# Single-stream layer: the down product by seven half-size products, with the residual added by pairs of tiles

## The reference, cut to what matters

```python
def swiglu(h, w_gate, w_up, w_down):
    return (jax.nn.silu(h @ w_gate) * (h @ w_up)) @ w_down

x = x + token_mixing(x, ...)
h = rmsnorm(x, ffn_norm_g[l])
x = x + swiglu(h, ff_w_gate[0], ff_w_up[0], ff_w_down[0])   # l = 0
x = x + token_mixing(x, ...)                                 # l = 1, begins with rmsnorm(x)
```

## Time and profile before

| | |
|---|---|
| median of 3 runs | 3439.45 us (3438.46 to 3442.85) |
| the profiled execution | 3442.54 us |
| its span | 3440.5 us |
| TensorE busy | 3270.0 us, 95% |
| VectorE, ScalarE, POOL busy | 26%, 20%, 14% |
| mean granted TensorE clock | 0.963 of full |

### The profile page before, as it was taken

The page is one execution under the profiler, slowest core; times in us unless marked ns, Lnnn a source line. Parts: engine busy times, 40 slices in busy tenths (PEclk is TensorE's granted clock), DMA queues, the critical chain, the costliest instruction groups (busy, mean ns, idle before and its releaser), DMA issues.

```text
span 3440.5 us, 81881 instructions
## 1 busy us (share of the span) xinstructions
PE 3270.0 (95%) x35194; PEld 2864.3 (83%) x35195; DVE 897.4 (26%) x1990; ACT 691.1 (20%) x1505; POOL 495.7 (14%) x441
## 2 busy tenths in 40 slices
PE   7999789999899999999999999989999999999998
PEld 5886678888786788787799887778899999988888
DVE  2324745553313321214233123130000110011001
ACT  2324122221204321212211011201111211101011
POOL 1210125555121010100057010000000000000000
PEclk9999689999899999999999999989999999999999
DMA  6546012222233244343344442238999999944477
GB/s 274 198 165 233 3 49 83 88 85 88 72 104 123 88 157 137 125 141 110 110 160 156 150 147 98 97 124 338 381 380 396 388 394 378 402 151 149 143 271 290
DMA packets 94204, 638.90 MB, mean 186 GB/s; under 512 B 10720, under 2 KB 11760, under 8 KB 36480
## 3 DMA queue, kind: packets, MB, share of 16 engines
q1 hardware_dynamic: 91472, 628.62, 49.2%
q0 software_dynamic: 2608, 8.49, 0.8%
HBM read 636.02 MB, written 1.05 MB: 185 GB/s over the span
## 4 chain that ended last, share of the span: by engine, by line
PE 89%; DMA 4%; DVE 3%; ACT 2%; issue 2%; POOL 0%; SPq 0%; ACTq 0%; DVEq 0%
PE bank L1109 18%; PE bank L663 18%; PE bank L618 12%; PE bank L781 12%; PE bank L802 5%; PE bank L634 5%; PE bank L719 4%; PE bank L1069 2%; DMA ring<-in_moe_down 2%; PE bank L566 2%; PE bank L592 1%; PE bank L1124 1%; PE bank L838 1%; DMA ring<-in_moe_up 1%; PE bank L820 1%
## 5 line engine op out<-in xcount | busy, mean ns | idle before, releaser
L781 PE MATMUL bank<-PROJ,ring 128*64 128x80 f32 (+1 forms) x7424 | 485.0, 257 | 11.6 <-DMA ring<-in_moe_down 7.7
L1109 PE MATMUL bank<-MIX,ring 128*64 128x80 f32 x12544 | 473.7, 235 | 21.1 <-issue 10.9
L1109 PEld LDWEIGHTS bank<-MIX,ring 128*64 128x64 f32 x12544 | 448.6, 138 | 47.0 <-issue 39.7
L781 PEld LDWEIGHTS bank<-PROJ,ring 128*64 128x64 f32 (+1 forms) x7424 | 441.8, 145 | 53.5 <-DMA ring<-in_moe_down 12.5
L618 PE MATMUL bank<-H,ring 128*128 128x256 f32 x1856 | 407.5, 382 | 4.1 <-ACT H L1297 4.1
L618 PEld LDWEIGHTS bank<-H,ring 128*128 128x128 f32 x1856 | 354.4, 192 | 56.7 <-issue 4.7
L1109 PE MATMUL bank<-H,ring 128*128 128x256 f32 x896 | 193.7, 379 | 0.0
L663 PE MATMUL bank<-H,ring 128*64 128x128 f32 (+1 forms) x1296 | 185.2, 331 | 5.4 <-ACT H L1297 4.7
L1109 PEld LDWEIGHTS bank<-H,ring 128*128 128x128 f32 x896 | 170.2, 190 | 23.4 <-issue 0.3
L663 PE MATMUL bank<-MIX,ring 128*64 128x128 f32 (+1 forms) x1272 | 181.1, 321 | 0.8 <-DVE MIX L1884 0.8
L802 PE MATMUL bank<-H,ring 128*128 128x256 f32 x768 | 178.0, 390 | 3.9 <-ACT PROJ L1396 3.7
(11 more groups left out here) (383 smaller groups left out, 3717.4 us busy)
## 6 DMA issues: line engine op xcount, KB each, us to landing
ring<-in_moe_up SPq DMA_DIRECT2D x224, 1024.0 KB, 7.2
ring<-in_moe_down SPq DMA_DIRECT2D x128, 896.0 KB, 6.3
ring<-in_up SPq DMA_DIRECT2D x44, 1024.0 KB, 4.8
ring<-in_mod_b SPq DMA_DIRECT2D x40, 1024.0 KB, 6.5
ring<-in_tproj SPq DMA_DIRECT2D x32, 1024.0 KB, 4.8
ring<-in_proj SPq DMA_DIRECT2D x26, 1024.0 KB, 4.8
ring<-in_gates SPq DMA_DIRECT2D x24, 1024.0 KB, 4.8
ring<-in_swup SPq DMA_DIRECT2D x22, 1024.0 KB, 4.8
```

Source lines behind the costliest of these rows:

```text
L781: mm = pe.matmul(B[bank][lo:lo + m, 0:width], w[:, k, lo:lo + m], src(s * half + k), start=s == 0 and k == 0, stop=s == 1 and k == half - 1)
L1109: mm = pe.matmul(B[(t0 + 2 * j + t) % 4][lo:lo + m, 0:n], w[:, k, t * P + lo:t * P + lo + m], src[:, k, 0:n], start=k == 0, stop=k == KT - 1)
```

## The change

`swdown` joins the stages by seven: 12 units of 1024 KB instead of 16 of 704 KB. VectorE makes the token sums of chunks 0 and 1 before the last gating, chunk 2's after it. POOL makes the weight sums two units ahead. ScalarE copies out the four lone products, in one loop before the squares of norm 10. VectorE combines each pair of tiles and adds it to X in one operation of 512 columns, and the square sums stand at fixed places between. The squares of norm 10 move from H to SC, where they share four places (`square_home`), with a wait on the fourth and later squares (`square_free`).

```diff
-SEVEN = ('proj0', 'wout0', 'up0', 'down0', 'proj1', 'swup')
+SEVEN = ('proj0', 'wout0', 'up0', 'down0', 'proj1', 'swup', 'swdown')
...
-DOWNS = ('down0',)
+DOWNS = ('down0', 'swdown',)
...
                     seven("swup", "norm9_out")
-                    down("swdown", T, ("lin_free", tile_base["swup"] + 2 * FT + 4, 2))
+                    seven_down("swdown")
...
                     sqrt_table(eps)
+                    for j in range(4):
+                        seven_head("swdown", j)
                     squares(10, X, T, lin_free, tile_base["swdown"] + 5, 1)
...
                         c_sums(name, j, it)
+                        if j == FT - 1:
+                            down_sums("swdown", (0, 1))
...
-                    add_out(10, "swdown")
+                    down_sums("swdown", (2,))
+                    for j in range(4):
+                        c_sums("swdown", j)
+                        dve.wait_ge(S("sv_c"), result_at("swdown") + j + 1)
+                        x = X[:, 2 * j:2 * j + 2, 0:T]
+                        dve.tensor_tensor(x, x, flat(seven_parts("swdown", j)[0]).rearrange("p (k t) -> p k t", t=T), ALU.add)\
+                           .then_inc(lin_free, 2)
+                        for k in ((), (1,), (2, 3), (4, 5))[j]:
+                            sum_square(10, k, T)
+                    sum_square(10, 6, T)
...
                             sums_ahead("swup", j, it)
+                    for j in range(2):
+                        pool.wait_ge(unit_done, base["swup"] + FT - 1 + j)
+                        w_sums("swdown", j)
+                    for j in range(10):
+                        sums_ahead("swdown", j)
```

More of the change, by code:

```diff
@@ L28 @@
 MOD_A = 8
-SEVEN = ('proj0', 'wout0', 'up0', 'down0', 'proj1', 'swup')
-SEVEN_UNITS = {'proj0': 11, 'wout0': 4, 'up0': 22, 'down0': 12, 'proj1': 4, 'swup': 22}
-SEVEN_WIDTH = {'proj0': 512, 'wout0': 512, 'up0': 512, 'down0': 512, 'proj1': 512, 'swup': 256}
+SEVEN = ('proj0', 'wout0', 'up0', 'down0', 'proj1', 'swup', 'swdown')
+SEVEN_UNITS = {'proj0': 11, 'wout0': 4, 'up0': 22, 'down0': 12, 'proj1': 4, 'swup': 22, 'swdown': 12}
+SEVEN_WIDTH = {'proj0': 512, 'wout0': 512, 'up0': 512, 'down0': 512, 'proj1': 512, 'swup': 256, 'swdown': 256}
 CHUNKS = ((0, 4), (4, 4), (8, 3))
-DOWNS = ('down0',)
+DOWNS = ('down0', 'swdown',)
 MOD_P = 22
@@ L2080, in add_out @@
                         sum_square(n, k - 1, T)
[L2081 to L2086, removed]
+                    bank = B[(tile_base[name] + k) % 4]
+                    dve.wait_ge(*tile_in(name, k))
                     dve.tensor_tensor(X[:, k, 0:T], X[:, k, 0:T], bank[:, 0:T], ALU.add).then_inc(lin_free, 1)
@@ L2470, in layout @@
     out["swup"] = paired(f["ff_w_gate_2"][0], f["ff_w_up_2"][0])
-    out["swdown"] = down(f["ff_w_down_2"][0])
+    out["swdown"] = down_seven(f["ff_w_down_2"][0])
     out["moe_up"] = np.concatenate([paired(f["moe_w_gate_2"][0][e], f["moe_w_up_2"][0][e]) for e in range(N_EXPERTS)])
```

## The result

The changed kernel takes 3450.42 us (median of 6 runs, 3445.17 to 3452.65), the kernel before 3439.44 (median of 6, 3437.68 to 3448.09). The ratio is 1.0026, with a 95% interval of 1.0014 to 1.0038: slower, by 11 us between the medians (5 to 13 by the interval). Forecast was 3438.8 with a range up to 3445.0. The profiled execution took 3445.17 us, the shortest of the six, with a span of 3443.4.

What follows compares the result with a forecast made beforehand. TensorE was taken to bound the kernel, with 89% of the chain. Its work -8.9, the start +2.2 and the end +6.0 gave -0.7 us: 3438.8 us against the median of 3439.45, range 3432.5 to 3445.0.

Steps and rivals of the forecast that it cites:

- TensorE's work, -8.9 us: Single-stream down product: 1232 instructions at 54.6 ns, 67.2 us against 76.08, so 8.9 us less.
- Transfers: Down product's weights: 12 transfers of 1024 KB for 16 of 704 KB, each started early enough; no cost.
- POOL in steady state: Down product: POOL's weight sums keep up with at least 0.7 us to spare, so no wait.
- Rivals 3 and 4: Down product: POOL falls behind, 3444.9 us, chance 0.04; strips do not run side by side, 3505 us, chance 0.01.
- The start, +2.2: Down product's first units: VectorE's token sums take turns with POOL's weight sums and delay TensorE, 2.2 us more; bounds 0 and 4.
- The end, +6.0: Down product's end to small gates' end: late squares hold up VectorE's combinations, E + 18.0 against E + 11.95; bounds 3 and 7.
- rival 1, "ScalarE not late": Rival 1: stage's end or start is cheap, chance 0.24; its case of ScalarE not late at the end: 3435.8 us.
- The sum, -0.7: Whole kernel: work, start and end terms together make it 0.7 us faster, 3438.8 us against the median.
- Rival 2: New stage's straight code: instructions come too late, 9 issue waits add 19 us, 3458 us; chance 0.05.

Runs made afterwards that it cites:

- f3: Changed kernel, padding branched over and ScalarE's squares in turn, plus POOL's second-unit weight sums waiting for VectorE's chunk 0 sums: 3436.61 us, ratio 0.9988.
- e3: Changed kernel with ScalarE's lone copies and squares in turn, instead of all copies first: 3447.95 us, ratio 1.0021.
- e2: Kernel before the change, with 60 slots of redundant waits (120 waits) added on TensorE ahead of the router: 3457.85 us, ratio 1.0044.
- e1: Changed kernel with TensorE branching over the alignment padding ahead of the experts' loop: 3436.38 us, ratio 0.9989.
- g1 to g3: Changed kernel with 15, 28 or 40 small products (60, 112, 160 slots) added before the first modulation tile: 3445.39, 3439.81, 3438.22 us.
- g3: Changed kernel with 40 small products (160 slots) added before the first modulation tile: 3438.22 us, ratio 0.9995.

## Why the prediction was wrong

**TensorE's work, -8.9 us: right.** The new stage, undisturbed, goes on at the forecast pace. With the start's cost the span from the gate/up stage's first product to E is 205.5 us, before 212.34: 6.85 less, forecast 6.7 less.

**Transfers, POOL in steady state: right.** The waits of TensorE in the stage are two of 0.6 us for VectorE's sums at the start; none is for POOL or a transfer. Rivals 3 and 4 did not happen.

**The start, +2.2: right in size and cause.** From its first product to E the stage takes 69.3 us, 2.1 more than the 67.2 of undisturbed work. VectorE's sums lasted 1.65 us where 1.66 was forecast from the turns; f3 shows that they are turns.

**The end, +6.0: right in cause, and in size partly by luck.** Measured 17.9 us from E against 18.0, but the means started 4.5 us after E where 5.1 was forecast, and the small gates took 9.15 us where 8.80 was: two misses of about half a microsecond that cancel. e3 confirms that ScalarE's order makes some 2.6 us of it, where the prediction had 3.0 (its rival 1, "ScalarE not late").

**The sum, -0.7: right for the stage (-0.93), wrong for the kernel.** The step that failed is that the sum ended there. It held the terms between the gate/up stage and the small gates, and silently took all the rest for unchanged. The rest was not unchanged. It held +9.7 us at the entry of the experts' loop, of which no term, no rival and no bound spoke. That e2 makes the same 11.86 us in the old kernel, and e1 and g1 to g3 take them away in the new one, shows the cause. With the filling brought back near that of before (g3), the ratio is 0.9995 (0.9986 to 1.0004), -1.7 us with an interval of some 3 us on either side: the forecast of -0.7 lies in it.

**Rival 2 was the near miss.** "Instructions come too late; slower" had 0.05, but put the cost in the new stage's straight code, by fetching, at 19 us. No issue wait of 2 us stands there. It was instruction supply, at another place and by another mechanism: slots run through, not code fetched late. The page "Runtime: NRT & Kernel Launch" of the Trainium skill (Instruction fetch mechanics) has the prefetch as sequential and hidden by the pace of issue, with a stall at a taken branch whose target is not loaded yet. By it the filling, which is straight code, should cost no fetch time, and in the first wait the trace agrees: 11.86 us without a transfer of instructions. The second wait fits the stall: between L1137 and the first product the kernel has an `If` whose other part is the one that runs, and a block of code lands inside the wait, 2.1 us ahead of the first product in the changed kernel. That the branch asks for that block is not shown.

**Smaller things in the profiled execution.** 3.4 us were won behind the stage, where the granted clock differs. At the gather the changed kernel was 4.3 us ahead, so the 9.7 us of the entry put it 5.4 us behind at the first expert's product; it was 6.4 us behind at the second gather and 2.9 at the end of the span. The median of the runs is 11 us above before, more than this one execution shows. The runs without profile carry no waits, so how the 5 us between this execution and the median are made up stays open. e1 lies 14.0 us under the changed kernel by the medians, 8.3 by the spans.

The chance of "slower" was 0.09. The one step that would have caught it was at hand before any run: the alignment stands in the printed code, and the slots ahead of it can be counted in both programs. The count alone (a shift of 60 modulo 256) leaves open whether the filling shrinks by 60 or grows by 196, since that depends on p, and no row of before has the price of a slot. But it is a rival with a place, and it would have moved the range upwards.

## What to carry to other kernels

A sum over the stage that a change touches is complete only if nothing behind it depends on the length of the code: look for alignments and loop entries downstream on the same engine, and count the slots ahead of them in both versions, in the compiled list. When a kernel gets slower and the changed stage has not, compare the traces landmark by landmark to the end, look at the "issue" waits, and try the suspected cause on the kernel before as well. An alignment's filling is best branched over before other changes are judged: then this down product, with ScalarE's squares in turn, gave 3432.6 us, 0.23% below the kernel before.

## What the runs showed of the hardware

- Slots of filling that are run through cost 73 ns each on TensorE's queue here (11.86, 7.40, 3.63 us at 60 and 52 slots' distance). Some 35 + p of them show in no wait; that they are run through while the gather's products are still running is an inference.
- No instruction transfer falls into those first waits, so the 73 ns are the running through and not the fetching.
- A redundant wait costs 46 ns: 320 in 14.81 us. Two share one slot.
- A float32 product takes four slots of TensorE's list, a transposition two: the two of L1137 show as x2, 40 small products as x80.
- VectorE's sum of 512 columns takes 0.69 us alone and 1.65 beside POOL's sums; POOL's takes 1.28 alone and 1.60. The turns that the earlier trace rows showed at 1024 columns hold at 512.
- The second wait at the entry (6.06, 3.71, 5.08, 5.78, and 2.56 with the filling branched over) does not follow the filling: the changed kernel and e3 have one and the same list on TensorE and show 3.71 and 4.84. Where the filling is run through, a 16 KB block of instructions lands in it, and the first product follows 2.1 to 2.3 us later. What sets when its transfer starts (0.3 to 2.9 us into the wait), and what the remaining 2.1 to 2.6 us are, stays open; a register load and a branch stand there in the code.
- Runs of one kernel spread by 4 to 10 us here (0.1 to 0.3%). Part of this may be TensorE's clock, which fell in one execution and stayed up in another over the same work; that was not tested.
